# Two-part rounded products of weights and values in a mixer's attention, three of its weight units on GpSimd, and the feed-forward's last gate and up columns as one job

## The chip, the cores and the metric

The kernel runs on one core of one Trainium2 chip. The metric is the device time of one execution in microseconds (us), the median over several runs. Everything below is on that one core: TensorE (PE, matmuls; PEld its weight loads), VectorE (DVE), ScalarE (ACT), GpSimd (POOL) and SyncE (SP, which issues the weight DMAs).

## The reference, cut to what matters

The network works on one sequence of 256 tokens with 1024 features, in f32. A first block of two layers (a gated linear attention, a differential attention and two mixtures of experts) is left as it is. A second block follows, twice over:

```python
for l in range(DEPTH):                       # DEPTH = 2
    x = layer_norm_2(ALPHA * x + 0.5 * swiglu(x, ffn1_gate[l], ffn1_up[l], ffn1_down[l]), ...)
    proj = x @ w_in[l]                       # split into h_a b_a c_a uv q kc vc ksl vsl kw vw gl
    y_a = short_conv(h_a, b_a, c_a, conv_w[l])
    y_b = gmlp_spatial(uv, ...)
    y_c = nsa_attention(q, kc, vc, ksl, vsl, kw, vw, gl, ...)
    x = layer_norm_2(ALPHA * x + concatenate([y_a, y_b, y_c]) @ w_out[l], ...)
    x = layer_norm_2(ALPHA * x + 0.5 * swiglu(x, ffn2_gate[l], ffn2_up[l], ffn2_down[l]), ...)

def swiglu(x, w_gate, w_up, w_down):         # 1024 -> 2816 -> 1024
    return (silu(x @ w_gate) * (x @ w_up)) @ w_down
```

The attention has 8 query heads of 64 features over 2 key heads. For each query three results are added, each times a gate: attention over 15 compressed keys, over chosen blocks and over a window. With 256 tokens the last two see all earlier tokens, each with keys and values of its own (ksl, vsl and kw, vw).

## The kernel before, in words

**Units and jobs.** All weights come in units of up to 128 x 2048 f32 (1 MB). `plan_cols` cuts a column range into units, one unit being so many k tiles (of 128 rows) by so many columns; the units that make one product are a job. SyncE loads unit after unit into 7 slots (`load_units`). Each f32 matrix is split in two rounded parts for TensorE's one-pass type fp32r: ScalarE writes the high part Whi (L414, 4 slots, `round_units`), and VectorE subtracts it to get the low part Wlo (L426, `rest_units`). For a few units (`pool_units`, 6 in the kernel) GpSimd does that subtraction (L434, `rest_unit_pool`). The input X is split the same way (XTh, XTl), and `use_unit` multiplies three times for each k tile: high by high (L477), high by low (L480), low by high (L485), for two token tiles t of 128. `job_pe`, `job_act` and `job_dve` walk through a job's units on each engine and yield after each, z = 0, 1 and so on; code that has to run there stands in the caller. After each yield, or before it, ScalarE and VectorE go on to round and subtract up to NS = 4 units ahead.

**Feed-forward** (`ffn_pe`, `ffn_act`, `ffn_dve`, four times in all). The 2816 columns are 5 chunks of 512 and one of 256 (`CH`). For chunk c there is a job for the gate and one for up. A job of 512 columns has two units of 4 k tiles; each of the two jobs of the last chunk has one unit of 8 k tiles by 256 columns. ScalarE takes SiLU of the gate out of PSUM (L850), VectorE multiplies it by up (L880), TensorE transposes the result of chunk c behind the first unit of chunk c + 1 (`turn`, L596), and both engines split it (L604, L608). Then follow two down jobs.

**Mixer** (`mixer_pe`, `mixer_act`, `mixer_dve`, `mixer_pool`, class `Mixer`, two layers). Its jobs are kv, q, kw, uv, ca, cb and out, with 2, 2, 2, 2, 2, 1 and 4 units. out's units come in the order k tiles 4 to 7 for both halves of the columns, then k tiles 0 to 3 for both. Attention work stands by hand between the units. There are 4 items (key head g, token tile t); `turn_(i)` runs `values(i - 2)`, `flip(i - 1)` and `scores(i)`. turn_(0) and turn_(1) stand behind uv's two units, 2 and 3 behind ca's, 4 behind cb's, and 5 after `gmlp()`. An item goes through these steps:
- `scores`: TensorE, rounded products of queries with split keys (L2508, L2509) and a mask (L2510); VectorE the row maxima (L2903); ScalarE the exponentials (L2709); VectorE scales them by the gates (`weights`, L2911 to L2920).
- `flip`: TensorE transposes the weights (L2524) in groups of four blocks, two groups for t = 0 and four for t = 1. The groups are copied to wT as f32, every first one by VectorE (L2929), every second by ScalarE (L2721).
- `values`: TensorE multiplies V (columns of P) by wT in plain f32, 512 moving columns, two matmuls for t = 0 and four for t = 1 (L2538), adds the compressed part with four matmuls of 128 moving columns (L2542), and ScalarE copies the half of the partitions that belongs to head g to OT (L2731).

The tail is `gmlp()` (L2560, L2968), `conv()` (L2570, L2981 to L2996), the splits of OT (XTh L2747; XTl L3047 on VectorE for t = 0, L2409 on GpSimd for t = 1), of the conv result (L2751, L3002) and of the gMLP result (L604, L608), and the out jobs, which `outer_pe` runs as unit 0 for both t, then units 1, 2, 3 for t = 0, then for t = 1. `outer_dve` calls what stands at z = 0 and only then goes on to subtract units. In `job_dve`, VectorE has by default subtracted out's second unit after ca's first, the third after ca's second, the fourth after cb.

Engines wait by semaphores; `on(name)` is the point at which the named result is ready. Each engine works its program strictly in order.

Of the kernel before, what the change touches and what calls it, by code (L numbers as in the profile page):

```python
# [132 lines left out]
def build(nc, A, cst_d, out):  # L133
# [253 lines left out]
    pool_units = {jobs[BEFORE[v]][-1] + 2 for v in POOL_AT}  # L387

# [422 lines left out]

    def ffn_pe(pe, a, l, v, split=True):
# [10 lines left out]
        for c in range(6):  # L823
# [14 lines left out]
    def ffn_act(act, a, l, v, split=True):  # L838
# [4 lines left out]
        for c in range(6):  # L843
            n, name = CH[c][1] - CH[c][0], ("fgate", a, l, c)

            def gate(t, b):
# [5 lines left out]
                free(act_done, name, t)  # L852
# [5 lines left out]
            for z in job_act(act, ("fup", a, l, c), None):  # L858
# [9 lines left out]
    def ffn_dve(dve, a, l, v, split=True):  # L868
# [5 lines left out]
        for c in range(6):  # L874
            n, name = CH[c][1] - CH[c][0], ("fup", a, l, c)

            def up(t, b):
                dve.wait_ge(*on("sg", a, l, c, t))
                dve.wait_ge(*product(name, t))
                dve.scalar_tensor_tensor(hd[:, t, 0:n], sg[:, t, 0:n], 0.5, PS[b][:, 0:n], ALU.mult,  # L880
                                         ALU.mult).then_inc(dve_done, tick(dve_done, "hd", a, l, c, t))
                free(dve_done, name, t)
            for z in job_dve(dve, ("fgate", a, l, c), None, skew=c == 0):
# [4 lines left out]
            for z in job_dve(dve, name, up):  # L888
                pass
# [1457 lines left out]

    class Mixer:
        def __init__(self, l):
# [12 lines left out]
            self.vcz = area("mx_vcz", [128, 8, 128])  # L2362
# [9 lines left out]
            self.wT = at_(f"mx_wT{l}", [128, 16, 128], f32, sh_o)  # L2372
# [11 lines left out]
    def mixer_pool(pool, l, v):  # L2384
# [9 lines left out]
        for j in range(2):  # L2394
# [20 lines left out]
    def mixer_pe(pe, l, v):  # L2415
# [112 lines left out]
        def values(i):  # L2528
            g, t = ITEMS[i]
            nbl = 2 * (t + 1)  # L2530
            b = bank(pe, "mo", l, i)
            for rr in heads(t):
                pe.wait_ge(*on("wts", l, i, rr[0]))
            w = M.wT[:, 0:4 * nbl, :].rearrange("p (r n) q -> p n r q", n=nbl)
            for n in range(nbl):
                m, k = n // (t + 1), n % (t + 1)
                c = 2176 + 256 * m
                pe.matmul(PS[b][:, :], P[:, k, c:c + 128], w[:, n], start=n == 0, stop=False)  # L2538
            pe.wait_ge(*on("wcs", l))
            pe.wait_ge(*on("vcs", l))  # L2540
# [664 lines left out]
```

## Time and profile before

| | |
|---|---|
| median of 3 runs | 1866.82 us (1862.39 to 1869.23) |
| the profiled execution: its own time, span | 1860.8 us, 1859.0 us |
| busy in the span | PE 1828.6 (98%), DVE 1300.8 (70%), ACT 1013.9 (55%), POOL 114.5 (6%) |
| granted TensorE clock, mean | 0.997 |
| subtractions on VectorE, units of 2048 columns (L426) | 370 of 2.29 us |
| roundings on ScalarE, units of 2048 columns (L414) | 376 of 1.92 us |
| units on GpSimd (L434) | 6 of 5.02 us |
| DMA | 426.56 MB, mean 229 GB/s |

How to read it: busy times of matmuls overlap, since a matmul counts until its last result is out. So what a matmul costs is read from the distance of starts. A plain f32 matmul stands as two records, a rounded one as one. The layers of the second block repeat themselves: the first mixer's attention lies between 1085 and 1155 us, the second's between 1582 and 1651 us. A wait stands in brackets behind the row that waited, with what ended it.

### The profile page before, as it was taken

What the parts mean: (1) busy time and instruction counts of PE and PEld (TensorE: products, weight loads), DVE (VectorE), ACT (ScalarE), POOL (GpSimd) and SP (SyncE); (2) the same over time, 40 slices, a digit from 0 to 9 for tenths busy, and PEclk for the clock granted to TensorE, in tenths of its full rate; (3) what the DMA queues carried; (4) which work ended last, traced back from release to release, by engine and by line L of the source; (5) the groups of instructions that cost most, each with busy time, mean ns of one, the idle gap of its engine ahead of it and who ended that gap; (6) DMA issues with size and microseconds to landing.
All of it is one profiled execution on the core that took longest, in us unless ns stands there. A gap on an engine that the chain in (4) does not pass through costs nothing.

```text
span 1859.0 us, 21830 instructions
## 1 busy us (share of the span) xinstructions
PE 1828.6 (98%) x9112; PEld 1530.7 (82%) x9112; DVE 1300.8 (70%) x1325; ACT 1013.9 (55%) x1083; POOL 114.5 (6%) x109
## 2 busy tenths in 40 slices
PE   8999999998999999999999999999999999999998
PEld 6788888888978888887888888888888888888886
DVE  5579989987789998997554667655465546876544
ACT  6547777774647777774443374544344434735431
POOL 1030000001010000000000300100010003020000
PEclk9999999999999999999999999999999999999999
DMA  9547999996436999996555642655565556346551
GB/s 347 170 160 272 356 366 356 367 364 205 142 134 241 356 371 356 358 371 230 188 192 167 209 164 91 227 181 170 192 220 187 170 192 209 125 149 210 185 170 57
DMA packets 220169, 426.56 MB, mean 229 GB/s; under 512 B 7560, under 2 KB 28304, under 8 KB 220064
## 3 DMA queue, kind: packets, MB, share of 16 engines
q1 hardware_dynamic: 214256, 406.93, 63.7%
q0 software_dynamic: 5808, 18.17, 3.1%
q8 instruction: 73, 1.20, 0.3%
q14 instruction: 32, 0.26, 0.0%
HBM read 424.01 MB, written 1.06 MB: 229 GB/s over the span
## 4 chain that ended last, share of the span: by engine, by line
PE 92%; DVE 5%; ACT 1%; issue 1%; POOL 0%; DMA 0%; POOLq 0%; DVEq 0%; SPq 0%
PE ps L485 27%; PE ps L477 25%; PE ps L480 25%; PE ps L596 2%; DVE Wlo L426 2%; PE ps L469 1%; PE ps L470 1%; PE ps L2538 1%; PE ps L1621 1%; PE ps L576 1%; PE ps L575 1%; PE ps L574 1%; PE ps L2439 1%; PE ps L2030 1%; PE ps L2524 1%
## 5 line engine op out<-in xcount | busy, mean ns | idle before, releaser
L426 DVE TENSOR_TENSOR Wlo<-raw,Whi 128x2048 fp32r<-128x2048 f32 (+2 forms) x387 | 865.4, 2242 | 406.4 <-ACT Whi L414 405.9
L414 ACT ACTIVATE Whi<-raw 128x2048 fp32r<-128x2048 f32 (+2 forms) x393 | 736.0, 1878 | 472.9 <-PE ps L485 468.1
L485 PE MATMUL ps<-Whi,XTl 128*128 128x512 f32 (+2 forms) x1496 | 549.2, 378 | 0.0
L477 PE MATMUL ps<-Whi,XTh 128*128 128x512 f32 (+2 forms) x1360 | 517.9, 381 | 8.3 <-DVE Wlo L426 8.0
L480 PE MATMUL ps<-Wlo,XTh 128*128 128x512 f32 (+2 forms) x1360 | 512.0, 376 | 0.0
L485 PEld LDWEIGHTS ps<-Whi,XTl 128*128 128x128 f32 x1496 | 281.4, 189 | 51.0
L477 PEld LDWEIGHTS ps<-Whi,XTh 128*128 128x128 f32 x1360 | 256.9, 189 | 55.6 <-DVE Wlo L426 8.0
L480 PEld LDWEIGHTS ps<-Wlo,XTh 128*128 128x128 f32 x1360 | 257.1, 189 | 44.3 <-issue 0.2
L477 PE MATMUL ps<-Whi,hTh 128*128 128x512 f32 x352 | 137.7, 391 | 0.0
L485 PE MATMUL ps<-Whi,hTl 128*128 128x512 f32 x352 | 137.1, 390 | 0.0
L480 PE MATMUL ps<-Wlo,hTh 128*128 128x512 f32 x352 | 137.1, 389 | 0.0
L477 PE MATMUL ps<-Whi,mo_hTh 128*128 128x512 f32 x256 | 101.0, 394 | 0.0
L477 PE MATMUL ps<-Whi,XGh 128*128 128x512 f32 x256 | 100.9, 394 | 0.0
L485 PE MATMUL ps<-Whi,mo_hTl 128*128 128x512 f32 x256 | 99.9, 390 | 0.0
L485 PE MATMUL ps<-Whi,XGl 128*128 128x512 f32 x256 | 99.9, 390 | 0.0
L480 PE MATMUL ps<-Wlo,mo_hTh 128*128 128x512 f32 x256 | 99.7, 390 | 0.0
L480 PE MATMUL ps<-Wlo,XGh 128*128 128x512 f32 x256 | 99.7, 389 | 0.0
L708 POOL TENSOR_TENSOR rs<-rs,cst 128x1 f32<-128x1 f32 x20 | 30.6, 1528 | 1072.8 <-DVE rs L700 1072.8
L485 PEld LDWEIGHTS ps<-Whi,hTl 128*128 128x128 f32 x352 | 66.1, 188 | 13.9
L477 PEld LDWEIGHTS ps<-Whi,hTh 128*128 128x128 f32 x352 | 66.1, 188 | 13.4
L480 PEld LDWEIGHTS ps<-Wlo,hTh 128*128 128x128 f32 x352 | 66.1, 188 | 13.3
L604 ACT ACTIVATE XTh<-ps 128x512 fp32r<-128x512 f32 (+1 forms) x44 | 23.8, 577 | 79.7 <-PE ps L596 79.5
(351 smaller groups left out, 2008.1 us busy)
## 6 DMA issues: line engine op xcount, KB each, us to landing
raw<-in_moe_w_gate SPq DMA_DIRECT2D x64, 1024.0 KB, 6.2
raw<-in_moe_w_up SPq DMA_DIRECT2D x64, 1024.0 KB, 6.6
raw<-in_moe_w_down SPq DMA_DIRECT2D x64, 1024.0 KB, 6.1
raw<-in_ffn_gate SPq DMA_DIRECT2D x44, 1024.0 KB, 5.1
raw<-in_ffn_up SPq DMA_DIRECT2D x44, 1024.0 KB, 5.1
raw<-in_ffn_down SPq DMA_DIRECT2D x40, 1024.0 KB, 5.0
raw<-in_w_in SPq DMA_DIRECT2D x18, 1024.0 KB, 5.2
raw<-in_a_w_in SPq DMA_DIRECT2D x10, 1024.0 KB, 13.1
```

Of the source, the lines that this page charges most:

```text
L414: act.activation(Whi[:, i % NS, 0:m * n], raw[:, i % NR, 0:m * n], ACT.Copy).then_inc(w_rounded, tick(w_rounded, "rounded", i))
L426: dve.tensor_tensor(Wlo[:, i % NR, 0:m * n], raw[:, i % NR, 0:m * n], h.bitcast(f32), ALU.subtract).then_inc(w_rest, tick(w_rest, "rest", i))
L469: pe.matmul(o, xh(k0 + q, t), h[:, q, :], start=k0 + q == first, stop=False)
L470: pe.matmul(o, xh(k0 + q, t), l[:, q, :], start=False, stop=False)
L477: pe.matmul(o, xh(k, t), h[:, q, :], start=k == first, stop=False)
L480: pe.matmul(o, xh(k, t), l[:, q, :], start=False, stop=False)
L485: x = pe.matmul(o, xl(k, t), h[:, q, :], start=False, stop=k == end)
L574: pe.matmul(o, h[:, q, c], XTh[:, q, :], start=q == 0, stop=False)
L575: pe.matmul(o, h[:, q, c], XTl[:, q, :], start=False, stop=False)
L596: x = pe.transpose(PS[b][:, q * 128:(q + 1) * 128], blk, cst[:, C_ID:C_ID + 128])
L604: act.activation(dst, src, ACT.Copy).then_inc(act_done, tick(act_done, "hi", *name))
L708: pool.tensor_tensor(rs[:, t, 1:2], rs[:, t, 0:1], cst[:, C_ONE + 1:C_ONE + 2], ALU.pow).then_inc(pool_done, tick(pool_done, "root", v, t))
```

## The change

Three parts.

1. The value products use rounded numbers in two parts. V is split: for each token tile k, kind m (chosen, window) and head g a 128-column matrix holds V's high part in columns 0 to 63 and its low part in 64 to 127, in place of columns of P that are no longer used. The weights are split too: ScalarE rounds all groups to wTh, VectorE subtracts all of them to wTl. Each old matmul becomes two, high weights and low weights, by the same two-part V. The product then has high V's result in one half of the partitions and low V's in the other, so ScalarE copies one half to OT and VectorE adds the other. The compressed part writes 64 partitions and moves behind the first matmul.
2. In each mixer layer GpSimd subtracts three units: ca's second, cb's and out's first. It loses the low part of OT for t = 1 to VectorE, which now takes it in `conv()`, and there out's second unit as well; out's third and fourth stand behind the splits of the conv and gMLP results.
3. The last 256 columns of gate and up are set side by side on the host, one array of 512 columns, and are one job of two units.

The diff, cut to its core:

```diff
-        for c, b in enumerate(CH):
+        for c, b in enumerate(CH[:5]):
             plan_cols(("fgate", a, l, c), A[f"{a}_gate_2"][l], *b)
             plan_cols(("fup", a, l, c), A[f"{a}_up_2"][l], *b)
+        plan_cols(("fboth", a, l), A[f"{a}_both"][l], 0, 512)
...
+    MIX_POOL = [[jobs["mx", l, "ca"][1], jobs["mx", l, "cb"][0], jobs["mx", l, "out"][0]] for l in range(2)]
+    pool_units.update(*MIX_POOL)
...
+        for z in job_pe(pe, ("fboth", a, l), xt_h, xt_l, ready):
+            if z == 0:
+                turn(4)
...
+                src = PS[b][:, 0:n] if c < 5 else PS[b][:, 512 - n:512]
+                dve.scalar_tensor_tensor(hd[:, t, 0:n], sg[:, t, 0:n], 0.5, src, ALU.mult,
...
-            self.vcz = area("mx_vcz", [128, 8, 128])
+            self.vcz = area("mx_vcz", [128, 8, 64])
...
-            self.wT = at_(f"mx_wT{l}", [128, 16, 128], f32, sh_o)
+            self.wTh = at_(f"mx_wTh{l}", [128, 16, 128], f32r, sh_o)
+            self.wTl = [at_(f"mx_wTl{l}{i}", [128, 16, 128], f32r, (B_o, Y_o)[i]) for i in range(2)]
...
     def mixer_pool(pool, l, v):
...
+        rest_unit_pool(pool, MIX_POOL[l][0])
+        rest_unit_pool(pool, MIX_POOL[l][1])
         pool.wait_ge(*on("gvar", l))
...
-        c = cols(4, 4, 1)
-        pool.wait_ge(*on("hi", "mo", l, 1))
-        pool.tensor_tensor(XTl[c], M.OT[:, 1], XTh[c].bitcast(f32), ALU.subtract).then_inc(
-            pool_done, tick(pool_done, "lo", "mo", l, 1))
+        rest_unit_pool(pool, MIX_POOL[l][2])
...
     # mixer_pe, values(i)
+            def chosen():
+                pe.wait_ge(*on("wcs", l))
+                pe.wait_ge(*on("vcs", l))
+                for r in range(4):
+                    pe.matmul(PS[b][0:64, r * 128:(r + 1) * 128], M.vcz[:, 2 * r + g, :], M.wcT[:, t, :], start=False,
+                              stop=False)
             for rr in heads(t):
-                pe.wait_ge(*on("wts", l, i, rr[0]))
+                pe.wait_ge(*on("lo", "wt", l, i, rr))
+            pe.wait_ge(*on("vs", l))
...
-                pe.matmul(PS[b][:, :], P[:, k, c:c + 128], w[:, n], start=n == 0, stop=False)
+                pe.matmul(PS[b][:, :], M.vs[k, m, g][:, :], wh[:, n], start=n == 0, stop=False)
+                if n == 0:
+                    chosen()
+                x = pe.matmul(PS[b][:, :], M.vs[k, m, g][:, :], wl[:, n], start=False, stop=n == nbl - 1)
...
     # mixer_act
+        def split_v():                       # called behind gates(), before the job uv
+            act.wait_ge(*on("twice", l, 1))
+            for m, c in ((0, 2176), (1, 2432)):
+                for k in range(2):
+                    for g in range(2):
+                        act.activation(M.vs[k, m, g][:, 0:64], P[:, k, c + 64 * g:c + 64 * g + 64], ACT.Copy).then_inc(
...
         def flip(i):
-            for rr in heads(t)[1::2]:
+            for rr in heads(t):
+                split_act(act, ("wt", l, i, rr), M.wTh[:, r0:r0 + 4, :], turned(("wt", l, i, rr), 4))
...
     # mixer_dve
         def flip(i):
-            for rr in heads(t)[0::2]:
+            for rr in heads(t):
+                split_dve(dve, n, M.wTl[i % 2][:, r0:r0 + 4, :], turned(n, 4), M.wTh[:, r0:r0 + 4, :])
+
+        def values(i):                       # called first in turn_(i + 2)
+            dve.wait_ge(*on("mo_part", l, i))
+            dve.tensor_tensor(M.OT[ps, t, :, :], M.OT[ps, t, :, :], turned(("mo", l, i), 4)[ps], ALU.add).then_inc(
+                dve_done, tick(dve_done, "mos", l, i))
+
+        def split_v():                       # called behind weights(0)
...
+                        dve.tensor_tensor(M.vs[k, m, g][:, 64:128], P[:, k, c + 64 * g:c + 64 * g + 64],
+                                          M.vs[k, m, g][:, 0:64].bitcast(f32), ALU.subtract).then_inc(
...
         def conv():
             dve.tensor_copy(M.zc[:, :, 2:258], PS[where[("conv", l, 0)]][:, :].rearrange("p (j n) -> p j n", n=256)
...
+            rest_o(1)
+            rest_units(dve, jobs["mx", l, "out"][1])
             for j in range(2):
...
-        for z in run("ca"):
+        for z in run("ca", upto=MIX_POOL[l][2]):
...
-        for z in run("cb"):
+        for z in run("cb", upto=MIX_POOL[l][2]):
             if z == 0:
                 turn_(4)
         conv_in()
+        rest_o(0)
         gmlp()
+        turn_(5)
         conv()
         for z in outer_dve(dve, v, ("mx", l, "out")):
             if z == 0:
                 split_y()
                 split_b()
...
+    for f in ("ffn1", "ffn2"):
+        inputs[f"{f}_both"] = np.concatenate([inputs[f"{f}_{k}_2"][:, :, 2560:] for k in ("gate", "up")], axis=2)
```

The comments "called ..." and the names of the functions between the parts are added here. `upto` keeps VectorE from going ahead of out's first unit in the jobs ca and cb; `rest_o(t)` is the low part of OT.

## Rows read from the trace of the kernel before

**Rows 1.** The page, part 4: the chain that ended last, shares of the span.

```profile
PE 92%; DVE 5%; ACT 1%; issue 1%; POOL 0%; DMA 0%; POOLq 0%; DVEq 0%; SPq 0%
```

**Rows 2.** Groups of instructions by line and form: names, shapes xcount | busy us, mean ns | idle.

```profile
L2538 PE MATMUL ps<-mx_wT,mx_P 128*128 128x512 f32 x48 | 22.0, 594 | 0.0
```

**Rows 3.** Timeline of TensorE, mixer layer 0: start us, length us, line, operation, tiles, xcount.

```profile
1115.34 0.39 PE L477 MATMUL ps<-Whi,XTh 128*128 128x512 f32 x1
...
1120.80 3.59 PE L2538 MATMUL ps<-mx_wT,mx_P 128*128 128x512 f32 x8
...
1128.32 0.28 PE L477 MATMUL ps<-Whi,XTh 128*128 128x256 f32 x1
...
1134.07 1.88 PE L2538 MATMUL ps<-mx_wT,mx_P 128*128 128x512 f32 x4
1135.79 1.05 PE L2542 MATMUL ps<-mx_wcT,mx_vcz 128*128 128x128 f32 x8
1136.68 1.91 PE L2524 MATMUL ps<-cst,mx_S 128*128 128x128 f32 x16
...
1138.42 1.90 PE L2560 MATMUL ps<-mx_P,mx_gw 128*128 128x64 f32 x16
1140.16 3.65 PE L2538 MATMUL ps<-mx_wT,mx_P 128*128 128x512 f32 x8
...
1144.54 1.04 PE L2570 MATMUL ps<-cst,mx_P 128*128 128x128 f32 x8
1145.44 0.50 PE L477 MATMUL ps<-Whi,XTh 128*128 128x512 f32 x1
...
1154.21 0.39 PE L477 MATMUL ps<-Whi,XTh 128*128 128x512 f32 x1
```

**Rows 4.** Timeline, layer 0: TensorE and ScalarE at item 0's scores; waits in brackets.

```profile
1092.10 0.35 PE L2508 MATMUL ps<-mx_kh,mx_qs 128*128 128x256 f32 x1 [0.52 <-DVE mx_kl L2848]
...
1093.99 0.41 ACT L2692 ACTIVATE mx_Sc<-mx_Sc 128x240 f32<-128x240 f32 x1 [1.76 <-DVE mx_Sc L2875]
```

**Rows 5.** Timeline of VectorE, mixer layer 0: item 3's weights and the tail.

```profile
1131.54 0.20 DVE L2911 RECIPROCAL mx_sm<-mx_sm 128x8 f32<-128x8 f32 x1 [2.03 <-ACT mx_S L2709]
...
1143.93 0.69 DVE L3047 TENSOR_TENSOR XTl<-mx_P,XTh 128x512 fp32r<-128x512 f32 x1
1144.53 1.62 DVE L2968 SCALAR_TENSOR_TENSOR mx_P<-ps,gbs,mx_P 128x64 f32<-128x64 f32 x8
1146.08 0.69 DVE L2981 COPY mx_zc<-ps 128x512 f32<-128x512 f32 x1
...
1146.80 0.71 DVE L2986 TENSOR_SCALAR mx_yc<-mx_zc,cw 128x256 f32<-128x256 f32 x1
...
1148.59 0.35 DVE L2986 TENSOR_SCALAR mx_yc<-mx_zc,cw 128x256 f32<-128x256 f32 x1
...
1150.09 0.88 DVE L2996 TENSOR_TENSOR mx_yc<-mx_yc,ps 128x256 f32<-128x256 f32 x2
1151.66 0.69 DVE L3002 TENSOR_TENSOR XTl<-mx_yc,XTh 128x512 fp32r<-128x512 f32 x1 [0.70 <-ACT XTh L2751]
```

**Rows 6.** Timeline: GpSimd's large subtractions, and a unit on VectorE beside one.

```profile
117.39 2.29 DVE L426 TENSOR_TENSOR Wlo<-raw,Whi 128x2048 fp32r<-128x2048 f32 x1
...
117.48 6.70 POOL L434 TENSOR_TENSOR Wlo<-raw,Whi 128x2048 fp32r<-128x2048 f32 x1 [1.53 <-ACT Whi L414]
...
1146.07 1.30 POOL L2409 TENSOR_TENSOR XTl<-mx_P,XTh 128x512 fp32r<-128x512 f32 x1 [23.26 <-ACT XTh L2747]
...
1164.63 4.68 POOL L434 TENSOR_TENSOR Wlo<-raw,Whi 128x2048 fp32r<-128x2048 f32 x1 [1.31 <-ACT Whi L414]
```

**Rows 7.** Stretches, TensorE: us, PE busy (xcount), granted clock (PEclk), DMA share, GB/s.

```profile
431.90:435.00 3.10, 0.18 (x2) 0.91 0.00 0
435.00:436.50 1.50, 1.45 (x7) 0.50 0.39 59
1093.20:1096.40 3.20, 3.20 (x10) 0.50 0.36 138
```

More of the change, by code:

```diff
@@ L822, in h_ready @@
             pe.wait_ge(*on("lo", "hT", a, l, k // 4, t))
-        for c in range(6):
+        for c in range(5):
             second = (lambda: second_pe(pe, v - 1)) if c == 0 else None
@@ L851, in gate @@
                     act_done, tick(act_done, "sg", a, l, c, t))
-                free(act_done, name, t)
+                if c < 5:
+                    free(act_done, name, t)
             for z in job_act(act, name, gate, skew=c == 0):
@@ L857, in ffn_act @@
                     turn(c - 1)
-            for z in job_act(act, ("fup", a, l, c), None):
+            for z in job_act(act, ("fup", a, l, c), None) if c < 5 else ():
                 pass
@@ L888, in ffn_dve @@
             for z in job_dve(dve, name, up):
-                pass
+                if c == 5 and z == 0:
+                    turn(4)
         for hf in range(2):
@@ L2687, in k_turn @@
                     act_done, tick(act_done, "kTs", l))
+        def split_v():
+            act.wait_ge(*on("twice", l, 1))
+            for m, c in ((0, 2176), (1, 2432)):
+                for k in range(2):
+                    for g in range(2):
+                        act.activation(M.vs[k, m, g][:, 0:64], P[:, k, c + 64 * g:c + 64 * g + 64], ACT.Copy).then_inc(
+                            act_done, tick(act_done, "vs_hi", l, m, k, g))
         def exp_cmp():
@@ L2729, in values @@
             act.wait_ge(*on("mo", l, i))
-            ps = slice(64 * g, 64 * g + 64)
-            act.activation(M.OT[ps, t, :, :], turned(("mo", l, i), 4)[ps], ACT.Copy).then_inc(
-                act_done, tick(act_done, "mos", l, i))
-            free(act_done, "mo", l, i)
+            ps, other = slice(64 * g, 64 * g + 64), slice(64 - 64 * g, 128 - 64 * g)
+            act.activation(M.OT[ps, t, :, :], turned(("mo", l, i), 4)[other], ACT.Copy).then_inc(
+                act_done, tick(act_done, "mo_part", l, i))
         def turn_(i):
@@ L2924, in flip @@
             g, t = ITEMS[i]
-            for rr in heads(t)[0::2]:
+            for rr in heads(t):
                 n = ("wt", l, i, rr)
                 r0 = rr[0] * 4 if t else rr[0] * 2
-                dve.wait_ge(*on(*n))
-                dve.tensor_copy(M.wT[:, r0:r0 + 4, :], turned(n, 4)).then_inc(
-                    dve_done, tick(dve_done, "wts", l, i, rr[0]))
-                for r in rr:
-                    point[("wts", l, i, r)] = point[("wts", l, i, rr[0])]
-                free(dve_done, *n)
+                split_dve(dve, n, M.wTl[i % 2][:, r0:r0 + 4, :], turned(n, 4), M.wTh[:, r0:r0 + 4, :])
+        def values(i):
+            g, t = ITEMS[i]
+            ps = slice(64 * g, 64 * g + 64)
+            dve.wait_ge(*on("mo_part", l, i))
+            dve.tensor_tensor(M.OT[ps, t, :, :], M.OT[ps, t, :, :], turned(("mo", l, i), 4)[ps], ALU.add).then_inc(
+                dve_done, tick(dve_done, "mos", l, i))
+            free(dve_done, "mo", l, i)
+        def split_v():
+            for m, c in ((0, 2176), (1, 2432)):
+                for k in range(2):
+                    for g in range(2):
+                        dve.wait_ge(*on("vs_hi", l, m, k, g))
+                        dve.tensor_tensor(M.vs[k, m, g][:, 64:128], P[:, k, c + 64 * g:c + 64 * g + 64],
+                                          M.vs[k, m, g][:, 0:64].bitcast(f32), ALU.subtract).then_inc(
+                            dve_done, tick(dve_done, "vs", l))
         def turn_(i):
+            if 0 <= i - 2:
+                values(i - 2)
             if 0 <= i - 1 < 4:
@@ L2976, in conv_in, with rest_o @@
                     dve_done, tick(dve_done, "z", l, t))
+        def rest_o(t):
+            c = cols(4, 4, t)
+            dve.wait_ge(*on("hi", "mo", l, t))
+            dve.tensor_tensor(XTl[c], M.OT[:, t], XTh[c].bitcast(f32), ALU.subtract).then_inc(
+                dve_done, tick(dve_done, "lo", "mo", l, t))
         def conv():
@@ L3044, in mixer_dve @@
         conv_in()
-        c = cols(4, 4, 0)
-        dve.wait_ge(*on("hi", "mo", l, 0))
-        dve.tensor_tensor(XTl[c], M.OT[:, 0], XTh[c].bitcast(f32), ALU.subtract).then_inc(
-            dve_done, tick(dve_done, "lo", "mo", l, 0))
+        rest_o(0)
         gmlp()
+        turn_(5)
         conv()
```

32 lines of the change are left out of this document (12 added, 20 removed).

## Prediction

> **What bounds the kernel now.** I read three views in this order. First the chain of work that ended last: 92% of the span is TensorE and only 5% VectorE [rows 1]. So a cut pays only where it takes time from TensorE's own queue, and only as long as TensorE does not then wait. Second, the groups of instructions by line: the value products of the mixer are 48 records, two for each of 24 plain-f32 matmuls (12 per mixer layer), with 512 moving columns [rows 2]. Third, the timeline of one mixer layer (layer 0; layer 1 repeats it), engine by engine, because the change shifts work between engines there. TensorE runs almost without a gap in it [rows 3]; its one named idle stretch is 0.52 us before the scores of item 0, for the low parts of the keys [rows 4]. VectorE and ScalarE have slack in most turns (2.03 us of waiting ahead of item 3's weights), but in the tail of the layer VectorE's operations follow each other with hardly a gap, and that decides this case [rows 5].
>
> **The sum, part by part.** Times are of the profiled execution (span 1859.0, whole 1860.8 us); the median of the three runs is 1866.8, 6.0 us above it, and I carry the difference over to the median.
>
> *Value products.* Four records of two f32 matmuls run from 1134.07 to 1135.79, 0.86 us a matmul. A rounded 512-column matmul takes 0.2275: 24 of them fill 1115.34 to 1120.80 [rows 3]. Each old matmul becomes two rounded ones, 0.455, so 0.405 is saved 24 times: **9.7 us** off TensorE. The matmuls of the chosen (compressed) part keep their 128 moving columns and fp32 type; four take 0.89 (1135.79 to 1136.68). Their stationary side is half as wide; no row shows f32 with 64 columns, so the bound is from nothing to 0.1 us an item, and I take nothing, as the moving side is unchanged. They now sit between rounded matmuls. The first rounded matmul after an f32 group starts about 0.1 late (after the transposes the first takes 0.34, 1145.44 and its 0.50 duration against 0.39): **+0.7** for 8 items, with bounds 0 and 1.
>
> *Feed-forward.* Per block, 96 matmuls with 256 columns become 48 with 512. 48 of 256 columns fill 1128.32 to 1134.07, 5.75 us [rows 3], so 11.50 becomes 48 x 0.2275 = 10.92; four blocks save **2.3 us**. The number and bytes of the weight units stay. SiLU and product now both come after the job, but their transposes follow only after the next job's first four k tiles (24 matmuls, 5.5 us), which covers the 0.4 and 0.4 us of the two engines. By the Trainium skill ("TensorE: Matmul & The Clock Gate", Back-to-back issue gap) only a fixed cost of some 2.5 ns a matmul would be spared, an estimate of 0.5 us instead of 2.3; the rows show about 12 ns a matmul and I go by them.
>
> *Work that GpSimd takes over.* It subtracts ca's second unit, cb's unit and out's first. VectorE sheds three of 2.29 us a layer; GpSimd needs 4.68, in one place 6.70 [rows 6]. The first is rounded before item 0's scores and due at 1115.34, the second is rounded before item 0 is transposed and due at 1128.32, the third due at 1145.44: each has about 10 us or more to spare, so they cost nothing. The root for the gMLP norm is queued behind the first two, and both are done before it is asked for; its DMAs come earlier or later in the queue than all three. With ca's unit off VectorE, the compressed keys and the low key parts come over 2 us sooner, and the 0.52 us wait goes: **-1.0** for two layers [rows 4].
>
> *Splitting V.* ScalarE adds 8 copies of 128x64, at about 0.2 us 1.6 us, in the 1.76 us in which it waits before the compressed exponentials [rows 4]. VectorE adds 8 subtractions, about 1.6, where cb's 2.29 stood. Nothing; without that cover up to 1 us a layer.
>
> *Splitting the weights.* Per layer ScalarE rounds all 12 groups instead of 6, and VectorE subtracts all 12 instead of copying 6. VectorE's next such operation starts 0.60 after the last (1143.93, 1144.53) [rows 5]. It also adds the second half of each value product (4 x 0.6) and the low part of output 1. In items 0 to 2 its waits for the exponentials (2.03 us in the turn with a row) and the shed units pay for that, so TensorE is not held. At item 3 it is.
>
> *The tail, where I look for the answer.* Count from the end of item 2's value product (before: 1136.68). TensorE then does 16 transposes 1.74, gMLP 1.74, item 3's product 8 x 0.2275 + 0.89 + 0.1 = 2.8 (before 3.49 + 0.89), conv transposes 0.9, and three out jobs with the two small transposes, 8.77 (1145.44 to 1154.21) [rows 3]: 16.0. The next matmul needs out's third unit. Before, VectorE had subtracted that unit before item 3 was even copied. Now it stands last, behind: the wait for ScalarE's half 0.8; add 0.6; four low parts 2.4; two products 0.7; wait for ScalarE 0.6 (an estimate: four roundings and a unit of weights stand ahead of its half); low of output 0 0.6; gMLP 1.6 (1144.53 to 1146.08); wait and add 0.9; copy 0.7; wait and low of output 1 0.8; out's second unit 2.2; conv taps 4.2 (1146.80 to the end of the 0.88 at 1150.09) less 0.4, below; wait for the rounding 0.7; low parts 0.6 and, for two of half size, 0.7; the third unit 2.3 [rows 5]. That is 20.0. Item 3's low parts are late too: they end at 0.8 + 0.6 + 2.4 and some latency, 4.0, where TensorE would take them at 3.5: 0.5. So TensorE arrives at 16.5 and waits **3.5 us a layer**. Total stalls: 2 x (3.5 + 0.5) = **+8.0**. The 0.4 taken off: while GpSimd ran the low part of output 1 (1.30 from 1146.07), VectorE's first tap took 0.71 and its twin 0.35 [rows 5, 6]; GpSimd no longer works there.
>
> *The clock.* After 3.1 us with almost nothing on TensorE, it worked from 435.00 at a granted 0.50 (1.2 instead of 2.4 GHz). After the 0.52 us wait of layer 0, 3.2 us went at 0.50; the same place in layer 1 shows none [rows 4, 7]. In the half clock the 3.2 us did 1.6 us of work. I expect each new stall to cost one such stretch, part of it spent in the wait: 1.2 a layer, **+2.4** (bounds 0 and 3.4), and the old dip to go with its wait, **-1.7** (bounds -1.7 and 0).
>
> Sum: -9.7 + 0.7 - 2.3 - 1.0 + 8.0 + 2.4 - 1.7 = **-3.6 us**: 1857.2 in a profiled execution, 1863.2 at the median. The cheaper matmuls are real and the tail of VectorE gives most of it back.
>
> **Rivals.**
> *A, the whole gain arrives.* VectorE's tail keeps up: no stall, no new dip: -9.7 + 0.7 - 2.3 - 1.0 - 1.7 = -14.0, so 1852.8. For it: VectorE sheds 13.7 us in six units, and waited 2.03 us in the turn ahead of the tail [rows 5]. Against: the tail above has hardly a free slot and out's second and third units moved into it. Between A and the forecast lie smaller stalls; half of them would give 1858.
>
> *B, slower: GpSimd holds VectorE.* Each GpSimd subtraction reads two operands. An operation of VectorE with two SBUF inputs that comes while it runs might wait to its end. Two places decide: V's low parts come just as cb's unit starts, the gMLP norm's second step just as out's starts. Each would wait some 4.7, less 1.4 of slack at the first: 8.0 a layer on VectorE's path and so on TensorE's, 16 us over the forecast: 1879. It decides once VectorE waits over about 1.4 us at V's split. For it: the 0.36 us that the first tap lost. Against: when both ran, the 2.29 us unit of VectorE was not lengthened and GpSimd's took 6.70 instead of 4.68 [rows 6]: GpSimd gave way. The Trainium skill ("SBUF — State Buffer", Who interferes with whom) says that an instruction of VectorE with two SBUF inputs contends with a GpSimd one that reads SBUF, and that issue order decides who blocks, which speaks for B here; the rows have it only with VectorE first.
>
> *C, no net effect.* The change does as it says, but each stall costs a full dip and the old dip stays: -3.6 + 1.0 + 1.7, and a second stretch at half clock after each stall +3.4: +2.5, 1869.3. That the rounded products don't run at the rounded rate (0.86 stays, twice as many: +20) I hold for excluded, since the scores are such products and fill no such time.
>
> **Chances.** A measurement of this kernel can tell about 0.5% (9.3 us) from no change. Forecast with its smaller and larger stalls 0.67; A 0.17; B 0.07; C 0.09. Faster by over 0.5%, below 1857.5: A and a slice of the forecast, 0.22. Slower, above 1876.1: B and a little of C, 0.08. Same: 0.70. Range: from A's 1852.8, taken in since it holds 0.17, to C's 1869.3; beyond lie B and the far ends of A, under 0.2. 1852 to 1870.
>
> **What would show it.** Right: value-product groups of rounded 512-column matmuls at 0.23; a TensorE wait of 3 to 4 us on VectorE's subtraction before out's third unit, in both layers, with granted clock 0.5 behind it; no wait at item 0's scores; the three units on GpSimd at 4.7 to 7 us. Wrong: TensorE's idle total no larger than before (A), V's subtractions or the norm's steps at many times their length while GpSimd is busy (B), or TensorE waiting in turns 1 to 3 on the weights' low parts, which I costed at nothing.

## The result and the profile after

The changed kernel takes **1873.29 us** (median of 10 runs, 1872.36 to 1874.16); the kernel before, in ten runs on the same chips, 1861.55 (1858.62 to 1869.23). The ratio is 1.0057 (95% interval 1.0046 to 1.0069): 11.7 us slower, where I had forecast 3.6 us faster. The three runs of before that I had seen lay high: 1866.8 against the 1861.55 of ten. So the absolute number, 1863.2 forecast, is missed by 10.1 us, and the difference, which is what the forecast was about, by 15.3; the high base hides 5.3 of it.

The page of the profile of the changed kernel: the busy time of each engine, and the chain that ended last by engine.

```profile
PE 1826.0 (98%) x8920; PEld 1520.8 (81%) x8920; DVE 1317.9 (70%) x1357; ACT 1021.2 (55%) x1111; POOL 139.5 (7%) x113
...
PE 86%; DVE 9%; ACT 2%; DMA 1%; issue 1%; POOL 1%; POOLq 0%; DVEq 0%; SPq 0%; ACTq 0%
```

Against [rows 1] TensorE lost 6 points of the chain, and VectorE gained 4. Where TensorE waited, by line (view of waits, engine TensorE; waiter, releaser, total, times, longest):

```profile
PE ps L481 <- DVE Wlo L430: 15.3, 3, 8.1
PE ps L2544 <- DVE mx_S L2947: 6.2, 4, 1.8
...
PE ps L2565 <- DVE mx_wTl L612: 1.7, 2, 0.9
...
PE ps L481 <- DVE mx_P L2961: 0.6, 1, 0.6
```

In the same view of the kernel before, the first of these is one wait of 8.0 us (the program's start), the other three don't exist, and there were two of 0.5 us for the low parts of the keys [rows 4], which are gone. New in the two mixers: 7.2 us at out's third unit, 6.2 at the flips of items 1 and 3, 1.7 at item 3's value product, 0.6 at a PSUM bank, less 1.0: 14.7 us.

First, the groups that answer to [rows 2], the value products and their compressed part:

```profile
L2544 PE MATMUL ps<-cst,mx_S 128*128 128x128 f32 x96 | 15.1, 299 | 6.3 <-DVE mx_S L2947 6.2
L2568 PE MATMUL ps<-mx_wTl,mx_vs 128*128 128x512 f32 x24 | 10.3, 428 | 0.0
L2565 PE MATMUL ps<-mx_wTh,mx_vs 128*128 128x512 f32 x24 | 9.6, 400 | 1.7 <-DVE mx_wTl L612 1.7
L2557 PE MATMUL ps<-mx_wcT,mx_vcz 128*64 128x128 f32 x64 | 8.7, 279 | 0.0
```

Second, TensorE's timeline at item 3's value product and at out's third unit in layer 0 (start, duration; answers to [rows 3]):

```profile
1142.00 0.47 PE L2565 MATMUL ps<-mx_wTh,mx_vs 128*128 128x512 f32 x1 [0.88 <-DVE mx_wTl L612]
1142.40 1.09 PE L2557 MATMUL ps<-mx_wcT,mx_vcz 128*64 128x128 f32 x8
1143.42 0.50 PE L2568 MATMUL ps<-mx_wTl,mx_vs 128*128 128x512 f32 x1
1143.75 0.39 PE L2565 MATMUL ps<-mx_wTh,mx_vs 128*128 128x512 f32 x1
1143.98 0.40 PE L2568 MATMUL ps<-mx_wTl,mx_vs 128*128 128x512 f32 x1
...
1158.44 0.50 PE L481 MATMUL ps<-Whi,XTh 128*128 128x512 f32 x1 [3.59 <-DVE Wlo L430]
```

The rounded products do run at 0.23, and the wait at out's third unit, forecast at 3.5 us, is 3.59. What the sum had not got stands on the timelines of GpSimd and VectorE in layer 0, at V's split and at the gMLP's norm (layer 1 repeats it: 5.59 and 4.76 us):

```profile
1098.65 4.63 POOL L438 TENSOR_TENSOR Wlo<-raw,Whi 128x2048 fp32r<-128x2048 f32 x1 [7.36 <-ACT Whi L418]
...
1123.69 4.58 POOL L438 TENSOR_TENSOR Wlo<-raw,Whi 128x2048 fp32r<-128x2048 f32 x1
```

```profile
1098.59 5.59 DVE L2970 TENSOR_TENSOR mx_vs<-mx_P,mx_vs 128x64 fp32r<-128x64 f32 x8
1104.11 1.28 DVE L612 TENSOR_TENSOR mx_wTl<-ps,mx_wTh 128x512 fp32r<-128x512 f32 x2
...
1123.82 4.75 DVE L3000 SCALAR_TENSOR_TENSOR mx_P<-mx_P,rs,mx_glg 128x256 f32<-128x256 f32 x1 [0.68 <-POOL rs L2428]
1128.48 0.47 DVE L2996 SCALAR_TENSOR_TENSOR mx_P<-mx_P,mv,mx_glg 128x256 f32<-128x256 f32 x1
1128.99 0.48 DVE L3000 SCALAR_TENSOR_TENSOR mx_P<-mx_P,rs,mx_glg 128x256 f32<-128x256 f32 x1
```

Read each pair across: an operation of 0.48 us (its twin at 1128.99) takes 4.75 us when GpSimd began 0.13 us before it, and it ends 0.3 us after GpSimd does. The eight operations of V's split at 1098.59 take 5.59 us in place of the 1.6 forecast. The same group, read from two narrower windows (the seven operations from 1098.73 on, the six from 1103.29 on), tells where:

```profile
1098.73 5.46 DVE L2970 TENSOR_TENSOR mx_vs<-mx_P,mx_vs 128x64 fp32r<-128x64 f32 x7
...
1103.29 0.89 DVE L2970 TENSOR_TENSOR mx_vs<-mx_P,mx_vs 128x64 fp32r<-128x64 f32 x6
```

The first began 0.06 us before GpSimd and passed. The second, begun at 1098.73, lasted to about 1103.3, where GpSimd's ends (1098.65 and 4.63); the other six then took 0.89. GpSimd's 4.63 and 4.58 are its own length (4.68 in [rows 6], 4.61 and 4.62 in run 1 below). This looks like rival B of the prediction. The profile counts the held time as busy time of the held operation, so that VectorE's share still reads 70%: no idle time tells of it, only a length far over that of a twin.

Last, the clock (view of windows, granted clock third from the right; answers to [rows 7]):

```profile
1092.60:1096.40 3.80, 3.80 (x18) 3.16 (x17) 3.43 (x10) 3.42 (x17) 0.00 (x0) 1.00 0.39 153
1110.80:1114.30 3.50, 3.32 (x17) 3.12 (x18) 3.50 (x7) 3.14 (x5) 0.00 (x0) 0.57 0.23 87
1158.50:1162.00 3.50, 3.50 (x10) 2.73 (x11) 3.50 (x2) 0.00 (x0) 0.00 (x0) 0.58 0.72 270
1660.60:1664.00 3.40, 3.07 (x7) 2.48 (x8) 3.40 (x3) 0.00 (x0) 0.00 (x0) 0.54 0.87 294
```

The stretch at 1.2 GHz behind the scores is gone; three others stand behind new waits: at item 1's flips in layer 0, and at out's third unit in both layers. Each lasts 3.4 us at 0.50 (1111.3 to 1114.8, 1159.0 to 1162.6 and 1660.8 to 1664.3, so it runs on a little past the window shown), and some 1.7 us of work are lost.

From the transposes of X in front of a mixer to those of its result, a mixer took 122.00 and 120.37 us before and takes 128.31 and 128.19 now: +14.1 together. The other blocks between such marks gained 2.2 together. The sum, 11.9, is the difference of the spans (1870.9 and 1859.0).

### The profile page after: what moved, and what is told of

Same layout as the page of the kernel before. It is cut to its first block, busy times and chain, and to the rows that moved or that the text cites. A ratio compares the mean times of both kernels' runs of the same rounds, so it can differ in the third digit from the quotient of the medians.

```text
span 1870.9 us, 21510 instructions
## 1 busy us (share of the span) xinstructions
PE 1826.0 (98%) x8920; PEld 1520.8 (81%) x8920; DVE 1317.9 (70%) x1357; ACT 1021.2 (55%) x1111; POOL 139.5 (7%) x113
## 4 chain that ended last, share of the span: by engine, by line
PE 86%; DVE 9%; ACT 2%; DMA 1%; issue 1%; POOL 1%; POOLq 0%; DVEq 0%; SPq 0%; ACTq 0%
PE ps L489 25%; PE ps L481 24%; PE ps L484 24%; DVE Wlo L430 2%; PE ps L600 2%; ACT mx_S L2742 1%; PE ps L473 1%; PE ps L474 1%; DVE mx_wTl L612 1%; PE ps L1632 1%; PE ps L580 1%; PE ps L579 1%; PE ps L578 1%; PE ps L2459 1%; DVE mx_vs L2970 1%
## 5 line engine op out<-in xcount | busy, mean ns | idle before, releaser
L430 DVE TENSOR_TENSOR Wlo<-raw,Whi 128x2048 fp32r<-128x2048 f32 (+2 forms) x381 | 851.1, 2241 | 396.5 <-ACT Whi L418 395.9
L489 PE MATMUL ps<-Whi,XTl 128*128 128x512 f32 (+2 forms) x1432 | 538.2, 387 | 0.0
L481 PE MATMUL ps<-Whi,XTh 128*128 128x512 f32 (+2 forms) x1296 | 507.9, 392 | 16.1 <-DVE Wlo L430 15.3
L484 PE MATMUL ps<-Wlo,XTh 128*128 128x512 f32 (+2 forms) x1296 | 501.4, 387 | 0.0
L489 PEld LDWEIGHTS ps<-Whi,XTl 128*128 128x128 f32 x1432 | 268.8, 189 | 53.9
L481 PEld LDWEIGHTS ps<-Whi,XTh 128*128 128x128 f32 x1296 | 244.8, 189 | 66.7 <-DVE Wlo L430 16.2
L484 PEld LDWEIGHTS ps<-Wlo,XTh 128*128 128x128 f32 x1296 | 245.1, 189 | 46.8 <-issue 0.2
```

The source lines that it names most:

```text
L430: dve.tensor_tensor(Wlo[:, i % NR, 0:m * n], raw[:, i % NR, 0:m * n], h.bitcast(f32), ALU.subtract).then_inc(w_rest, tick(w_rest, "rest", i))
L481: pe.matmul(o, xh(k, t), h[:, q, :], start=k == first, stop=False)
L484: pe.matmul(o, xh(k, t), l[:, q, :], start=False, stop=False)
L489: x = pe.matmul(o, xl(k, t), h[:, q, :], start=False, stop=k == end)
```

## The experiments

Theory H (hold): a GpSimd subtraction that has begun keeps VectorE's operations with two SBUF inputs waiting, and that is the loss. Theory T (tail): the rest is VectorE's order in the tail, as forecast, and the clock behind it. Rivals: added VectorE work in itself (W), or both engines slowing each other whenever they run side by side (B in the expectations, not the rival B of the prediction, which is H). Below, a meeting is a place where a GpSimd subtraction and such a VectorE operation fall together. Three chips were used for the runs, each with the kernel before beside them; its medians there (1862.02, 1862.22, 1861.62) lie within 0.6 us.

**1. No overlap.** The kernel after, and two waits for GpSimd:

```diff
         rest_unit_pool(pool, MIX_POOL[l][0])
+        pool.wait_ge(*on("vs", l))
         rest_unit_pool(pool, MIX_POOL[l][1])
...
+        pool.wait_ge(*on("gn", l, 1))
         rest_unit_pool(pool, MIX_POOL[l][2])
```

> GpSimd starts cb's unit only when VectorE has split V, and out's first unit only when VectorE has made the second half of the gMLP's norm; nothing else is changed against the kernel after. Theory H (a GpSimd subtraction that has begun keeps VectorE's operations with two SBUF inputs waiting to its end, 4.0 us at V's split and 4.3 us at the norm in each layer): the eight split operations go back from 5.59 us to about 1.6, the norm's from 4.75 us to 0.48, TensorE's waits for the weights of items 1 and 3 (1.78 and 1.2 us) go, and about 7.2 us a layer come back: 14 us less than the kernel after, near 1859, some 3 us below the kernel before. The 3.6 us wait at out's third unit stays. Theory W (what costs is the added work on VectorE and the order of the tail, not the meeting of the two engines): within 2 us of the kernel after, near 1873, since no work is taken away. Theory B (both engines share the SBUF and slow each other whenever they run side by side): less than half comes back, since the units then run beside other VectorE work, 1867 or more.

Measured 1862.24 us, ratio to before 0.9999 (0.9989 to 1.0009). VectorE's timeline at the two places:

```profile
1100.70 1.17 DVE L2972 TENSOR_TENSOR mx_vs<-mx_P,mx_vs 128x64 fp32r<-128x64 f32 x8
...
1123.52 0.48 DVE L3002 SCALAR_TENSOR_TENSOR mx_P<-mx_P,rs,mx_glg 128x256 f32<-128x256 f32 x1 [0.68 <-POOL rs L2429]
...
1124.84 0.67 DVE L2963 TENSOR_TENSOR mx_P<-mx_P,ps 64x512 f32<-64x512 f32 x1
1125.43 1.27 DVE L612 TENSOR_TENSOR mx_wTl<-ps,mx_wTh 128x512 fp32r<-128x512 f32 x2
1126.63 2.46 DVE L2932 TENSOR_REDUCE mx_nm<-ps 128x2 f32<-128x512 f32 x4
```

and GpSimd's:

```profile
1101.95 4.61 POOL L438 TENSOR_TENSOR Wlo<-raw,Whi 128x2048 fp32r<-128x2048 f32 x1 [8.55 <-DVE mx_vs L2972]
...
1125.00 4.62 POOL L438 TENSOR_TENSOR Wlo<-raw,Whi 128x2048 fp32r<-128x2048 f32 x1 [1.58 <-DVE mx_P L3002]
```

The split is back at 1.17, the step at 0.48, and TensorE's waits at the flips are gone, with the same work on each engine. 11 us of the kernel after came back. W falls, since no work was taken away. B falls too: from 1125.00 on GpSimd runs beside three groups of VectorE with an operand in PSUM, and no group is longer than alone. TensorE in the tail, item 3's transposes, which start where item 2's value product ends, and out's third unit:

```profile
1134.15 1.91 PE L2546 MATMUL ps<-cst,mx_S 128*128 128x128 f32 x16
...
1154.78 0.80 PE L481 MATMUL ps<-Whi,XTh 128*128 128x512 f32 x1 [3.63 <-DVE Wlo L430]
```

The time is 3 us over the expectation. In part that is clock: behind the tail's wait this kernel shows

```profile
1153.60:1160.60 7.00, 5.82 (x14) 4.62 (x15) 5.82 (x4) 0.00 (x0) 0.34 (x1) 0.52 0.40 152
1652.10:1655.70 3.60, 3.00 (x7) 2.42 (x8) 3.60 (x3) 0.00 (x0) 0.00 (x0) 0.53 0.81 281
```

some 10 us at the half clock, as much as the kernel after, although that kernel's stretch behind item 1's flips (1.7 us of work) is gone with the wait there. The trace is of the slowest of the twelve executions (1864.28), but the median of their mean granted clocks is 0.995 too, as in the kernel after, against 0.997 before. The other 1.5 us stay unexplained.

**2. No overlap at V's split alone.** Only the first of the two waits.

> Only the first of the two waits of the run above: GpSimd's cb unit starts after V's split, while out's first unit still meets the gMLP's norm. Theory H: TensorE's wait at item 1's flips goes (1.78 us plus transposes at half the clock), that at item 3's (1.2 to 1.5 us, and 1.1 at a bank) stays: 3.3 us a layer less than the kernel after, near 1866.7; the norm's step still 4.7 us long, the split back at 1.6. Theory W: as the kernel after, near 1873.

Measured 1870.38, ratio to before 1.0044 (1.0028 to 1.0060): 2.9 us of the kernel after's 11.7 by the medians, 4.0 by the spans. The split took 1.17, the norm's step still 4.75. The direction is H's; it gave less than the 6.6 expected, and the meeting at the norm, with 8.1 us from here to run 1, costs more than the one at V. In this trace the tail's wait of layer 0 again has 6.8 us at the half clock behind it, where the kernel after has 3.4.

**3. Who comes first.** GpSimd's cb unit is released by the first of VectorE's eight split operations, by `pool.wait_ge(*on("vs1", l))` in front of it.

> The kernel after, with GpSimd's cb unit released by the first of VectorE's eight split operations rather than before them. If the hold is taken anew at each instruction, GpSimd's unit begins 0.2 us later and the other seven operations wait for its 4.6 us: split 5.8 us, time 1873 to 1874. If VectorE keeps its turn while its operations stand back to back: split 1.6 us, GpSimd's unit shows 4.6 plus some 1.4 us, and about 3 us a layer come back, near 1867.

Measured 1869.61 (1865.78 to 1872.46), ratio 1.0037 (1.0025 to 1.0049). GpSimd and VectorE:

```profile
1100.38 5.36 POOL L438 TENSOR_TENSOR Wlo<-raw,Whi 128x2048 fp32r<-128x2048 f32 x1 [7.60 <-DVE mx_vs L2971]
```

```profile
1100.08 1.17 DVE L2971 TENSOR_TENSOR mx_vs<-mx_P,mx_vs 128x64 fp32r<-128x64 f32 x8
```

VectorE kept its turn: the operations left at 1100.38 were not delayed, and GpSimd's is 0.75 longer than the 4.61 of run 1, about what VectorE still had to do. This is the pattern of [rows 6], where VectorE's 2.29 us unit began first and GpSimd's took 6.70. But it is no rule for a row of small operations. Here GpSimd came 0.30 us into the row, when the third of the eight had just begun (1100.35), and the five behind it passed ahead of GpSimd; in the kernel after it came 0.06 us into the row, during the first, and got in ahead of the second. What decides inside a row stays open. For single operations, the runs show that the one which comes second waits; for both engines, that either can be the one that waits. The time came out 2.6 us over the 1867 expected. The trace, of the slowest of the six executions, has 17 us at 1.2 GHz in the mixers, run 2's 10, which would be 3.4 us; whether the median has them too is not shown.

**4. Smaller pieces.** GpSimd's three units as four instructions of 512 columns each.

> The kernel after with each of GpSimd's three mixer units subtracted in four instructions of 512 columns (1.15 us each by 4.6 / 4), at the same places. Theory H with a handover at each instruction's end: VectorE's operations wait for one piece at a time; V's split takes 1.6 plus 1.2 to 4.6 us, the norm's step 0.5 to 1.7 us, and 4 to 12 us of the kernel after come back: 1861 to 1869. If GpSimd's next piece always comes before VectorE's waiting one: split 5.6 and norm 4.7 us as in the kernel after, 1873 plus GpSimd's starts.

Measured 1871.35, ratio 1.0048 (1.0033 to 1.0063). GpSimd, the last piece having a line of its own, and VectorE:

```profile
1098.43 3.81 POOL L441 TENSOR_TENSOR Wlo<-raw,Whi 128x512 fp32r<-128x512 f32 x3 [6.94 <-ACT Whi L418]
1102.19 1.30 POOL L445 TENSOR_TENSOR Wlo<-raw,Whi 128x512 fp32r<-128x512 f32 x1
...
1123.46 4.13 POOL L441 TENSOR_TENSOR Wlo<-raw,Whi 128x512 fp32r<-128x512 f32 x3
```

```profile
1098.37 5.61 DVE L2980 TENSOR_TENSOR mx_vs<-mx_P,mx_vs 128x64 fp32r<-128x64 f32 x8
...
1123.59 1.44 DVE L3010 SCALAR_TENSOR_TENSOR mx_P<-mx_P,rs,mx_glg 128x256 f32<-128x256 f32 x1 [0.69 <-POOL rs L2438]
1124.95 1.50 DVE L3006 SCALAR_TENSOR_TENSOR mx_P<-mx_P,mv,mx_glg 128x256 f32<-128x256 f32 x1
1126.49 1.40 DVE L3010 SCALAR_TENSOR_TENSOR mx_P<-mx_P,rs,mx_glg 128x256 f32<-128x256 f32 x1
```

The engines now change places piece by piece. Each of VectorE's steps waits for one piece (1.4 instead of 4.75), but then so do the next two. The eight small operations gain nothing, 5.61: read from narrower windows, the second to the sixth begin at 1098.51, 1099.73, 1100.98, 1102.24 and 1103.50, so that one small operation gets through behind each piece. Cutting the unit up only spreads the hold: 2 us came back, not 4 to 12.

**5. The hold alone, in the kernel before.** GpSimd takes out's first unit directly after its root; nothing else of the change.

```diff
+    pool_units.update(jobs["mx", l, "out"][0] for l in range(2))
...
+        rest_unit_pool(pool, jobs["mx", l, "out"][0])
         c = cols(4, 4, 1)
         pool.wait_ge(*on("hi", "mo", l, 1))
```

> The kernel before, with one thing of the change: GpSimd, not VectorE, subtracts out's first unit in each mixer, directly after its root, where it meets the gMLP's norm. VectorE is spared 2.28 us a layer. Theory H: the norm's second step takes 4.75 us, not 0.48, 2.0 us more than VectorE is spared; item 3's weights come late, TensorE waits about 2 us a layer in all at item 3's flips and value product: 4 us slower than the kernel before, 3 to 8 with stretches at half the clock. If the hold needed the rest of the change: the same time as before, 1862.

Measured 1864.78, ratio 1.0022 (1.0009 to 1.0035): 3.2 us slower, though VectorE has 2.28 us a layer less to do. GpSimd, VectorE, and TensorE's new line in the view of waits:

```profile
1124.42 4.54 POOL L435 TENSOR_TENSOR Wlo<-raw,Whi 128x2048 fp32r<-128x2048 f32 x1
```

```profile
1124.54 4.70 DVE L2961 SCALAR_TENSOR_TENSOR mx_P<-mx_P,rs,mx_glg 128x256 f32<-128x256 f32 x1 [0.69 <-POOL rs L2406]
```

```profile
PE ps L2540 <- DVE mx_wT L2931: 2.3, 2, 1.2
```

So the hold arises without anything else of the change. The loss is within the expectation (4, 3 to 8); one of the ten executions, at 1876.45, lies far off the others (1863.14 to 1866.69).

**6. No units on GpSimd.** The kernel after, VectorE subtracting all units in the order of before.

> The kernel after without GpSimd's three mixer units: VectorE makes them again, in the order of before (2.28 us each, 6.8 us a layer more on VectorE), the value products and the feed-forward as after. Theory H: no hold of VectorE, but VectorE gets full: waits of TensorE of some 1.1 us at item 3's flips, 1.7 us for item 2's score bank and 3 us at item 3's value product, the 3.6 us at out's third unit gone: about 3.5 us a layer less than the kernel after, 1865 to 1868. Theory W (VectorE's load is the cost): 6.8 us more load a layer make it slower than the kernel after, 1878 or more.

Measured 1867.30, ratio 1.0028 (1.0018 to 1.0038), 6.0 us less than the kernel after with 6.8 us a layer more for VectorE. More work on VectorE, and yet faster: W falls a second time. But VectorE then is too full: in layer 0 TensorE waits 3.08 us for item 3's low weights, 1.37 for item 2's score bank and 1.13 at item 3's flips. So units on GpSimd are worth having, at the right moment.

**7. The feed-forward part alone** (kernel before, its hunks only).

> The kernel before with the feed-forward part of the change alone. Forecast in the sum: 2.3 us less (0.58 in each of four blocks), between 1.6 and 3 us less, 1859.2 on a base of 1861.5. If the part did nothing: 1861.5; if a new wait stood at the joint job: slower than before by up to 4 us.

Measured 1858.33, ratio 0.9979 (0.9970 to 0.9988): 3.7 us less by the medians, 2.2 to 5.6 by the interval, which just takes in the 2.3. The mixers of this trace took 120.42 and 120.43 us, 1.5 less together than before's: the half clock behind item 0's scores is not there, though the 0.51 us wait is. So 2.2 us are the part itself, and the rest is this clock.

**8. Out's second unit early.** Kernel 1, and in VectorE's `turn_(i)`:

```diff
             if i < 4:
                 scores(i)
+                if i == 3:
+                    rest_units(dve, jobs["mx", l, "out"][1])
                 weights(i)
```

> The first run (both GpSimd units kept clear of VectorE's work) and, with it, VectorE subtracts out's second unit in item 3's window, where it is idle for 2.04 us, and not in the tail before the taps. Theory T (TensorE's 3.63 us at out's third unit are VectorE's 2.28 us subtraction in front of the taps, and the waiting brings the stretches at half the clock that follow, 6.8 us in layer 0 and 3.4 us in layer 1, which cost half their length): the wait falls to about 1.3 us a layer, 4.6 us for both; with the stretches at half the clock gone 5.1 us more: 1852.5 to 1857.5, below the kernel before. Rival (the wait at the third unit is set by the landing or the rounding of that unit, not by VectorE's order): the wait stays at 3.6 us, time as the first run, 1862.

Measured 1853.96, ratio 0.9959 (0.9946 to 0.9973). The wait fell from 3.63 to

```profile
1151.26 0.50 PE L481 MATMUL ps<-Whi,XTh 128*128 128x512 f32 x1 [1.54 <-DVE Wlo L430]
```

and the mixers, 118.92 and 118.86 us, have no stretch at the half clock. Between the two traces 9.7 us were gained (by the medians 8.3): 4.2 are the wait, 5.1 the clock that it had brought.

**9. Out's third unit on GpSimd too**, behind item 3's weight products:

```diff
         rest_unit_pool(pool, MIX_POOL[l][2])
+        pool.wait_ge(*on("mw", l, 3, 3))
+        rest_unit_pool(pool, MIX_POOL[l][3])
```

> The run above, and GpSimd also takes out's third unit, from the end of item 3's four weight products on, while VectorE works on PSUM operands. By theory H the unit costs VectorE at most some 0.6 us (its end meets the convolution's input product), by theory T nothing waits at out's third unit: the mixers cost what they cost with the feed-forward part alone less 3.4 us for the value products and 0.7 us for the wait at the first scores, and 0.5 us more at item 3's value product: 3.6 us a layer below the 1858.3 of that run, 1851. If the third unit is not what TensorE waits for any more: as the run above.

Measured **1851.14** (1849.74 to 1852.00), ratio 0.9940 (0.9926 to 0.9953): below both kernels, and where it was expected. TensorE's view of waits has only the start's 8.0 us left on that line. The mixers took 117.05 and 117.02. GpSimd and VectorE around the new unit:

```profile
1133.72 4.55 POOL L438 TENSOR_TENSOR Wlo<-raw,Whi 128x2048 fp32r<-128x2048 f32 x1 [5.08 <-DVE mx_S L2951]
```

```profile
1128.04 2.75 DVE L430 TENSOR_TENSOR Wlo<-raw,Whi 128x2048 fp32r<-128x2048 f32 x1
...
1133.99 0.69 DVE L2965 TENSOR_TENSOR mx_P<-mx_P,ps 64x512 f32<-64x512 f32 x1 [0.36 <-ACT mx_P L2762]
1134.71 2.48 DVE L612 TENSOR_TENSOR mx_wTl<-ps,mx_wTh 128x512 fp32r<-128x512 f32 x4
1137.12 1.77 DVE L3022 TENSOR_TENSOR mx_P<-mx_P 128x256 f32<-128x256 f32 x2
```

Five operations with an operand in PSUM pass at their own length. The first with both in SBUF, at 1137.12, is held to GpSimd's end at 1138.27: the pair takes 1.77 instead of 0.75. VectorE's own unit at 1128.04, moved into item 3's window in run 8, meets the end of out's first unit on GpSimd (1124.02 to 1128.64) and takes 2.75 instead of 2.28. Neither makes TensorE wait.

**10. Item 3 copied first.** Kernel 9, with `flip(3)` in front of `values(2)` on ScalarE and VectorE.

> The kernel with out's third unit on GpSimd, and in the fourth turn after uv ScalarE and VectorE copy item 3's turned weights before they take over item 2's values, not after. Expected: the four low parts are there 0.6 us earlier (one 0.67 us addition of VectorE less in front of them), TensorE's last wait of the change, 0.53 us a layer at item 3's value product, goes: 1 us less, 1850. If the wait is set by TensorE's own flips: no difference, 1851.

Measured 1849.46 (1849.36 to 1850.07), ratio 0.9933 (0.9920 to 0.9947): the lowest time here, 0.5 us below its expectation, though its interval overlaps that of run 9. The wait at item 3's value product went from 0.53 to 0.25 us.

**11. The tail mended alone**: kernel 9 without the two waits of kernel 1.

> The kernel after with the tail mended alone: VectorE takes out's second unit in item 3's window and GpSimd out's third after item 3's weight products, while cb's and out's first unit still meet VectorE's operations as in the kernel after. If the two causes add: the meetings cost what the first run gave back, 11 us over the 1851 of the kernel with both mended, 1862, about the kernel before; TensorE's waits at the weights of items 1 and 3 stay, that at out's third unit is gone. If the late VectorE ate up what the tail gains: 1868 or more.

Measured 1862.92, ratio 1.0005 (0.9995 to 1.0014). As expected, TensorE's waits at the flips (6.1 us) and at item 3's value product (1.8) stay, and that at out's third unit is gone. The two causes add: the meetings cost 11.8 us with a mended tail and 11.1 without; the tail, 10.4 with the meetings and 11.1 without. These are differences of medians from different chips, so the 0.7 us between them mean nothing.

## Why the prediction was wrong

**The step that failed** is "each has about 10 us or more to spare, so they cost nothing", in *Work that GpSimd takes over*. I costed the units by when TensorE needs them, which was right: it never waited for one of them. But they take something from VectorE while they run: 4.4 us at V's split and 4.3 at the norm's step in each layer, which cost 11 to 12 us of the whole (runs 1 and 11). I had described exactly this as rival B, with both places and a price of 16 us over the forecast, and gave it 0.07. On the base of ten runs that is 1861.55 - 3.6 + 16 = 1873.9, and 1873.29 was measured. That they lie so near is luck: B's price is 4 to 5 us too high, and the other terms of the forecast, below, are 3.4 too low. Two things went wrong in the weighing. [rows 6] showed VectorE beginning 0.09 us ahead of GpSimd; I noted that the rows have it only so, and still counted "GpSimd gave way" against B as if it were a property of the engine. And the page of the Trainium skill that I cited ("SBUF — State Buffer", Who interferes with whom) names issue order as what decides; in the change GpSimd's out unit is queued right behind its own root, and the VectorE operation waits for that same root, so that GpSimd comes first (by 0.13 us, as measured). That order could be worked out from the code, with no run. At V's split it could not: there GpSimd starts on ScalarE's rounding, and came 0.06 us after the first of the eight. The measurements agree with the page: 4.75 us where GpSimd began first, nothing lost on the eight in run 3, where VectorE did, and nothing on operations with one operand in PSUM. Inside a row of VectorE's operations they are divided: run 3's row kept its turn to the end, the kernel after's lost it behind the first.

Point by point, for the rest:

- *Value products*, -9.7 + 0.7 = -9.0. The pitch was right (0.23), the switches undersized. From the traces of runs 7 and 1, by the distance of starts, values and compressed part: 2.60 and 4.32 us for an item of t = 0 and t = 1 became 2.14 and 3.06, so -3.4 a layer, **-6.9**. An item pays 0.09 at its first rounded matmul, 0.11 at the next behind the compressed part, and that part itself, for which I had taken nothing and looked only for a gain, takes 1.02 instead of 0.89 (1142.40 to 1143.42 above): 0.33 an item where I had 0.1.
- *Feed-forward*, -2.3: -2.2 between the marks of the two traces. Right, by the trace's 12 ns a matmul and not by the 2.5 of the Trainium skill ("TensorE: Matmul & The Clock Gate", Back-to-back issue gap), which would give 0.5.
- *Keys*, -1.0: the wait is gone, right.
- *Splitting V*, nothing: right without GpSimd (1.17 us for eight), 4.4 us more beside it.
- *The tail*, 3.5 us a layer: 3.59, with its reason shown by run 8; moving out's second unit alone took 2.1 of it. But the meetings had pushed TensorE and VectorE late alike, so this agreement alone would have proved little; run 1, without them, has 3.63. There TensorE arrives 17.0 us after item 2's value product and VectorE's third unit 20.6 (1134.15, and 1154.78 less its wait of 3.63, above), where I had 16.5 and 20.0: both legs are about half a microsecond short, and the difference came out so well because the two errors cancel.
- *Item 3*, 0.5: 0.53 without the meetings (run 1), 0.88 with them.
- *Clock*, +2.4 and -1.7. Together +0.7, and undersized: the mixers of the kernel after have three stretches at the half clock where before had one, +5.1 and -1.7, so +3.4; run 1 has as much. That the old stretch "goes with its wait" is not shown: it is gone in every trace without the wait, but it is absent in run 7 too, with the wait there, and stands in run 5's trace with the same wait. What sets it off stays open.
- *The meetings*, nothing: 6.2 us at flips, 0.6 at a bank, part of 1.7 at the value product, and transposes of items 1 and 3 that then go at the pace of VectorE's weight products (0.61 for each four) rather than TensorE's.

Without the meetings the forecast of -3.6 would have come to -0.2 (interval -2.0 to +1.7; run 1 against before). The switches (2.1) and the clock (2.7) more than account for the 3.4 between the two; the sum of 4.8 is over it by less than the interval's half.

## What to carry to other kernels

When work is given to GpSimd, cost it twice: by its own due time, and by which of VectorE's operations with both inputs in SBUF start while it runs; each of them can be held until GpSimd ends. Put the unit behind the last of these and in front of work that reads PSUM; here two waits of one line each did that and turned 1873 into 1862 us, and a further unit placed so held VectorE for only 1.0 us. And look at what an edit puts last in a stage: the tail, counted out operation by operation, had its wait foretold, each of the two chains to about half a microsecond, and mending it was worth about as much as the meetings.

## What was not expected of the hardware

- A held operation counts as busy, so no view of waits shows it: the 5.59 us at V's split appear as a wait of TensorE (1.78 us) on VectorE's weights of the next item.
- GpSimd too waits when it comes second (5.36 against 4.61 us), and with four pieces in a row the engines changed places at each piece: 1.40 to 1.50 us for an operation of 0.48 at the norm, and some 1.25 from one small operation to the next at V's split.
- A wait of TensorE of 3.6 us was followed by 3.4 us at 1.2 GHz in one layer and by 6.8 us in the same layer of another kernel; a wait of 1.54 us at the same place by none. In run 1's trace the clock took 5 us beside 7.3 us of such waits.
